# A score row copied later and value products in groups of four, in the stick-breaking attention of a streaming encoder step on one Trainium2 core

## What is computed

```python
def stick_breaking_block(q, k, v, q_pos, k_pos):
    z = jnp.einsum('bthd,bshd->bhts', q, k) * (SB_HEAD_DIM ** -0.5)
    mask = k_pos[None, :] < q_pos[:, None]
    log_fail = jnp.where(mask, jax.nn.log_sigmoid(-z), 0.0)
    after = lax.cumsum(log_fail, axis=3, reverse=True) - log_fail
    a = jnp.where(mask, jnp.exp(jax.nn.log_sigmoid(z) + after), 0.0)
    return jnp.einsum('bhts,bshd->bthd', a, v)
```

## Time and profile before

| | |
|---|---|
| median of 3 runs | 1090.89 us (1090.44 to 1092.22) |
| the profiled execution | 1091.26 us |
| its span, first to last instruction | 1089.4 us |
| mean granted TensorE clock | 0.995 |
| PE, DVE, ACT, POOL busy | 98%, 60%, 52%, 12% of the span |
| the stage of attention steps of the second pair | 241 to 325 us |

### The profile page before, as it was taken

How to read it: one execution, slowest core, us unless ns; L and a number is a source line. 1 busy time by engine, 2 the same in 40 slices (tenths; PEclk the granted TensorE clock), 3 DMA queues, 4 the chain that set the end, 5 groups by cost and what they waited for, 6 DMA issues and landing times.

```text
span 1089.4 us, 16617 instructions
## 1 busy us (share of the span) xinstructions
PE 1064.0 (98%) x6260; PEld 974.8 (89%) x6260; DVE 650.7 (60%) x1139; ACT 571.7 (52%) x1264; POOL 133.6 (12%) x145
## 2 busy tenths in 40 slices
PE   8999999999999999999999999999999999999995
PEld 5998779998779998779998779999999999999994
DVE  6677798387798377797387797335522231362117
ACT  4557884467883467883567884554022123252221
POOL 0001102011112011012011012001200110121220
PEclk9999999999999999999999999999999999999997
DMA  8041032132031132031142140153111111111144
GB/s 295 1 130 49 20 109 63 57 97 96 20 127 50 62 96 86 23 136 40 61 112 70 39 135 24 40 187 109 39 39 39 40 45 52 39 40 40 39 193 174
DMA packets 41487, 84.86 MB, mean 78 GB/s; under 512 B 2112, under 2 KB 22208, under 8 KB 41280
## 3 DMA queue, kind: packets, MB, share of 16 engines
q1 hardware_dynamic: 40832, 81.43, 22.9%
q10 hardware_dynamic: 576, 2.36, 0.6%
HBM read 67.27 MB, written 16.52 MB: 77 GB/s over the span
## 4 chain that ended last, share of the span: by engine, by line
PE 78%; ACT 9%; DVE 9%; issue 3%; DMA 1%; ACTq 0%; POOL 0%; DVEq 0%; SPq 0%; POOLq 0%
PE bank L671 50%; PE bank L1012 9%; DVE E L1676 3%; PE bank L808 3%; ACT E L1298 2%; ACT SPH L1310 2%; PE bank L838 2%; ACT E L1293 2%; DVE E L1680 1%; PE bank L794 1%; PE bank L681 1%; PE bank L708 1%; PE bank L912 1%; PE bank L954 1%; PE bank L976 1%
## 5 line engine op out<-in xcount | busy, mean ns | idle before, releaser
L671 PE MATMUL bank<-xh,wh 128*128 128x384 f32 x1296 | 438.8, 339 | 3.1 <-issue 2.8
L671 PE MATMUL bank<-xh,wl 128*128 128x384 f32 x1296 | 439.8, 339 | 0.0
L671 PE MATMUL bank<-xl,wh 128*128 128x384 f32 x1296 | 439.2, 339 | 0.0
L671 PEld LDWEIGHTS bank<-xh,wh 128*128 128x128 f32 x1296 | 243.6, 188 | 11.2 <-issue 9.3
L671 PEld LDWEIGHTS bank<-xh,wl 128*128 128x128 f32 x1296 | 243.6, 188 | 4.5 <-issue 2.0
L671 PEld LDWEIGHTS bank<-xl,wh 128*128 128x128 f32 x1296 | 243.5, 188 | 3.2 <-issue 0.2
L1183 ACT ACTIVATE slot<-bank,ngate 128x384 f32<-128x384 f32 x48 | 27.7, 576 | 177.9 <-PE bank L671 175.3
L1450 DVE CAST wh<-wr 128x1024 fp32r<-128x1024 f32 x64 | 43.7, 683 | 99.0 <-PE bank L671 98.1
L1455 DVE TENSOR_TENSOR wl<-wr,wh 128x1024 fp32r<-128x1024 f32 x64 | 90.8, 1419 | 1.9
L1676 DVE SCALAR_TENSOR_TENSOR E<-E,bank 128x512 f32<-128x512 f32 (+3 forms) x96 | 53.1, 553 | 47.7 <-ACT E L1298 47.6
L1858 DVE TENSOR_TENSOR slot<-bank,slot 128x384 f32<-128x384 f32 x24 | 13.4, 556 | 96.6 <-PE bank L1012 96.6
(11 more groups left out here) (226 smaller groups left out, 1687.0 us busy)
## 6 DMA issues: line engine op xcount, KB each, us to landing
wr<-wch SPq DMA_DIRECT2D x64, 512.0 KB, 3.6
KTc<-ckT SPq DMA_DIRECT2D x4, 2048.0 KB, 9.6
Vc<-cv SPq DMA_DIRECT2D x4, 2048.0 KB, 8.3
graw<-gated SPq DMA_DIRECT2D x8, 576.0 KB, 7.7
xres<-xT SPq DMA_DIRECT2D x1, 4608.0 KB, 15.7
yT<-yb SPq DMA_DIRECT2D x6, 576.0 KB, 3.0
xw<-xT SPq DMA_DIRECT2D x4, 768.0 KB, 11.6
okT<-kT ACTq DMA_DIRECT2D x4, 576.0 KB, 3.0
```

The lines of the kernel that those rows point to most:

```text
L671: i = nc.tensor.matmul(CH[n % 2][:, 0:WIN], weights[:, k, :], rows[:, k, w * WIN:(w + 1) * WIN], start=(m == 0), stop=(m == 23))
```

## The change

On ACT the copy of the score row leaves its place between exponential and logarithm. It now stands behind the high part of the softplus, waits for the softplus of its own step (`s_sp`, in steps without a high part too), and has a semaphore (`s_zr`), for which PE waits before it adds into the bank. The four row buffers `zr` become two tiles `zrows`, used at partitions 0 and 32 in turn; the high and low part of the carried row change places in `RT` in the same rhythm. In the space won, the weight tiles `Aw` go from three to five buffers; ACT waits for the value products of the step five before, and not three. PE makes the value products in groups of four, at steps 6, 10, 14, 18, 22 and 26, instead of groups of two at every even step from 4. The same instructions are issued, in other places; `s_hg` is waited for in five steps instead of two, at the same value.

```diff
--- before.py
+++ after.py
@@ -314,9 +314,9 @@
         SPH = [take(f"SPH{i}", [P, QW], F32R)[0] for i in range(2)]
         SPL = [take(f"SPL{i}", [P, QW], F32R)[0] for i in range(2)]
         RT = [take(f"RT{h}", [P, QW], F32R)[0] for h in range(2)]
-        zr = [take(f"zr{i}", [P, QW])[0] for i in range(4)]
-        aw_o = off[0] + 4 * QW
-        Aw = [take(f"Aw{i}", [P, QW])[0] for i in range(3)]
+        zrows = [take(f"zrows{i}", [P, QW])[0] for i in range(2)]
+        aw_o = off[0] + 3 * 4 * QW
+        Aw = [take(f"Aw{i}", [P, QW])[0] for i in range(5)]
 
         place = over(bt_o)
         Es = place("Es", [P, 2, SW])
@@ -426,6 +426,7 @@
         s_sp1 = sem("softplus_raw")
         s_sp = sem("softplus")
         s_S = sem("later_row")
+        s_zr = sem("first_key_row_copied")
         s_rz = sem("later_rows_zeroed")
         s_sph = sem("softplus_high")
         s_spl = sem("softplus_low")
@@ -514,6 +515,18 @@
         s_yo = sem("y_done")
         s_out = sem("y_stored")
 
+        def row_at(n):
+            return 32 * (n % 4 // 2)
+
+        def zr(n, cols):
+            return zrows[n % 2][row_at(n):row_at(n) + 1, cols]
+
+        def row_high(n, cols):
+            return RT[STEPS[n][2]][row_at(n):row_at(n) + 1, cols]
+
+        def row_low(n, cols):
+            return RT[STEPS[n][2]][32 - row_at(n):33 - row_at(n), cols]
+
         def need(eng, s, v):
 
             if v > 0:
@@ -811,9 +824,11 @@
                         if q == 0:
                             pe.wait_ge(s_cr, 3)
                             pe.wait_ge(s_sp, t + 1)
+                            pe.wait_ge(s_zr, SUMS * p + sums_until(m))
                             i = add(negtri, E[m % 2], c0)
                         else:
                             pe.wait_ge(s_sph, SPLITS * p + rows_until(m))
+                            pe.wait_ge(s_zr, SUMS * p + sums_until(m))
                             add(negtri_r[:, :], SPH[m % 2], c0)
                             pe.wait_ge(s_Sl, SUMS * p + sums_until(m - 2))
                             add(rows_r[:, :], RT[h], row_col(m - 2))
@@ -822,22 +837,21 @@
                         i.then_inc(s_cum, 1)
                     for x in B_PIECES[n][mid:]:
                         product(4 + 8 * p + x // 9, x // 3 % 3, x % 3)
-                    if n >= 4 and n % 2 == 0:
-                        wd, j, _ = STEPS[n - 4]
-                        c0 = first_col(n - 4)
-                        if n == 4:
+                    if n >= 6 and n % 4 == 2:
+
+                        if n == 6:
                             need(pe, s_oc, 3 * p)
                             pe.wait_ge(s_te, 6 * p + 3)
-                        if j == 4 * wd + 3:
-                            need(pe, s_gA, 2 * p + wd)
                         pe.wait_ge(s_a, NS * p + n - 2)
                         if diagonal(n - 3):
                             pe.wait_ge(s_am, DIAGS * p + diagonals_until(n - 3))
-                        for h in range(2):
-                            r = slice(DH * h, DH * h + DH)
-                            nc.tensor.matmul(OB[r, c0:QW], v_nat[:, j * P + DH * h:j * P + DH * h + DH],
-                                             Aw[(n - 4 + h) % 3][:, c0:QW], start=(j == 4 * wd + 3), stop=(j == 0),
-                                             skip_group_check=True).then_inc(s_av, 1)
+                        for m in range(n - 6, n - 2):
+                            wd, j, h = STEPS[m]
+                            c0, r = first_col(m), slice(DH * h, DH * h + DH)
+                            if j == 4 * wd + 3 and h == 0:
+                                need(pe, s_gA, 2 * p + wd)
+                            nc.tensor.matmul(OB[r, c0:QW], v_nat[:, j * P + DH * h:j * P + DH * h + DH], Aw[m % 5][:, c0:QW],
+                                             start=(j == 4 * wd + 3), stop=(j == 0), skip_group_check=True).then_inc(s_av, 1)
                     for w12 in ended(B_PIECES[n - 2]) if n >= 2 else ():
                         turn_recurrence(p, w12)
                 for w12 in ended(B_PIECES[-2]) + ended(B_PIECES[-1]):
@@ -1291,28 +1305,29 @@
                         elif n >= 2:
                             act.wait_ge(s_spl, SPLITS * p + rows_until(n - 2))
                         nc.scalar.activation(E[n % 2][:, c0:QW], ZB[n % 4][:, c0:QW], ACT.Exp).then_inc(s_E, 1)
-                        if STEPS[n][1] > 0:
-                            need(act, s_Sl, SUMS * p + (sums_until(n - 4) if n >= 4 else 0))
-                            nc.scalar.activation(zr[n % 4][0:1, row_col(n):QW], ZB[n % 4][0:1, row_col(n):QW], ACT.Copy)
                         act.wait_ge(s_E, t + 1)
                         nc.scalar.activation(E[n % 2][:, c0:QW], E[n % 2][:, c0:QW], ACT.Ln, bias=1.0).then_inc(s_L, 1)
                     if 2 <= n <= NS + 1:
                         m = n - 2
                         c0, t = first_col(m), NS * p + m
                         act.wait_ge(s_cum, t + 1)
-                        need(act, s_av, t - 2)
-                        if m < 2:
+                        need(act, s_av, t - 4)
+                        if m < 5:
                             need(act, s_hg, 3 * p)
-                        nc.scalar.activation(Aw[m % 3][:, c0:QW], ZB[m % 4][:, c0:QW], ACT.Exp).then_inc(s_a, 1)
+                        nc.scalar.activation(Aw[m % 5][:, c0:QW], ZB[m % 4][:, c0:QW], ACT.Exp).then_inc(s_a, 1)
                     if n < NS and tile_rank(n) > 0:
                         c0, t = first_col(n), NS * p + n
                         act.wait_ge(s_sp, t + 1)
                         nc.scalar.activation(SPH[n % 2][:, c0:QW], E[n % 2][:, c0:QW], ACT.Copy).then_inc(s_sph, 1)
+                    if n < NS and STEPS[n][1] > 0:
+                        act.wait_ge(s_sp, NS * p + n + 1)
+                        need(act, s_Sl, SUMS * p + (sums_until(n - 4) if n >= 4 else 0))
+                        nc.scalar.activation(zr(n, slice(row_col(n), QW)), ZB[n % 4][0:1, row_col(n):QW], ACT.Copy).then_inc(s_zr, 1)
                     if 2 <= n <= NS + 1 and STEPS[n - 2][1] > 0:
                         m, cols = n - 2, slice(row_col(n - 2), QW)
                         act.wait_ge(s_rz, 2 * (p + 1))
                         act.wait_ge(s_S, SUMS * p + sums_until(m))
-                        nc.scalar.activation(RT[STEPS[m][2]][0:1, cols], zr[m % 4][0:1, cols], ACT.Copy).then_inc(s_Sh, 1)
+                        nc.scalar.activation(row_high(m, cols), zr(m, cols), ACT.Copy).then_inc(s_Sh, 1)
                     recurrence_aside(p, n)
                     for w12 in ended(B_PIECES[n]):
                         window_recurrence(p, w12)
@@ -1512,16 +1527,15 @@
             def later_row(p, m):
 
                 cols = slice(row_col(m), QW)
-                row = zr[m % 4][0:1, cols]
+                row = zr(m, cols)
                 dve.wait_ge(s_a, NS * p + m + 1)
                 V.tensor_tensor(row, ZB[m % 4][0:1, cols], row, ALU.subtract).then_inc(s_S, 1)
 
             def later_row_low(p, m):
 
-                h, cols = STEPS[m][2], slice(row_col(m), QW)
+                cols = slice(row_col(m), QW)
                 dve.wait_ge(s_Sh, SUMS * p + sums_until(m))
-                V.tensor_tensor(RT[h][32:33, cols], zr[m % 4][0:1, cols], RT[h][0:1, cols].bitcast(F32),
-                                ALU.subtract).then_inc(s_Sl, 1)
+                V.tensor_tensor(row_low(m, cols), zr(m, cols), row_high(m, cols).bitcast(F32), ALU.subtract).then_inc(s_Sl, 1)
 
             def values_low(p):
 
@@ -1933,7 +1947,7 @@
                         m = n - 2
                         c0 = first_col(m)
                         pool.wait_ge(s_a, NS * p + m + 1)
-                        G.tensor_tensor(Aw[m % 3][:, c0:c0 + P], Aw[m % 3][:, c0:c0 + P], causal, ALU.mult).then_inc(s_am, 1)
+                        G.tensor_tensor(Aw[m % 5][:, c0:c0 + P], Aw[m % 5][:, c0:c0 + P], causal, ALU.mult).then_inc(s_am, 1)
                     for w12 in ended(B_PIECES[n]):
                         window_recurrence(p, w12)
```

## The result

The changed kernel takes **1117.1 us** (median of 4 runs, 1116.69 to 1117.58) against 1091.4 (1090.44 to 1092.22) for the kernel before on the same chip. The ratio is 1.0236, 95% interval 1.022 to 1.0251. The forecast was 1100.3, the range 1090.5 to 1105: the direction is right, the size is not. 25.7 us were lost where 9.4 were forecast.

What follows compares the result with a forecast made beforehand. ACT and DVE were taken to set the pace together from step 2 to 20, PE after. Per pair 0.68 + 0.67 + 0.40 + 0.29 + 0.3 = 2.34 us, 9.4 in four: 1090.89 + 9.4 = 1100.3 us, range 1090.5 to 1105.

Steps and rivals of the forecast that it cites:

- The sum of the late copy: Attention stage: copy +0.13 us net per step, plus waits; 2.04 us later per pair at step 20, 2.34 in all.
- The stall of steps 8 and 9: ACT: the late copy waits for the masked softplus; exponential 10 comes 1.35 us later, 0.67 of it new.
- the 0.6 for late low parts: Steps 21 and 25: PE arrives earlier and waits for the row's later low parts, 0 to 0.6 us, 0.6 taken.
- so I take the same price (bounds 0 and 0.1 us per row, off ACT's path): Rows at partition 32: same price as before, since the low part written there takes 0.68 against 0.67 us.
- each instruction overlaps the next by 0.10: ACT: the copy added behind the high part costs its duration minus 0.10 us, 0.47 at 512 columns.
- Behind step 20: PE -0.3: Value groups of steps 20 and 24 go, saving PE 0.3 us per pair that is sure to be time.
- The groups before step 20: Larger value groups there shorten PE where it waits for others; PE work falls 1.3 us per pair in the whole stage.
- a break costs: PE: a break between the two kinds of matmul costs 0.10 + 0.11 + 0.05 = 0.26 us.
- four records one behind the other at 0.23: PE: a group of two value products is four records, 0.92 us at the usual 0.23, of 1.01 measured.
- PE sets the pace: Rival: the saved breaks count whole, 5.4 us faster, 1085.5 us; chance 0.15.
- Worse than the sum: Rival: PE also waits for the copy before adds and for rows in steps 15 to 19; above 1104 us; chance 0.05.
- The signs I had named: Exponential to logarithm 0.60 us, copy waits 0.8 and 0.3, groups 1.97, PE waits +3.6 per pair, chunk 3's first window 2 later.

Runs made afterwards that it cites:

- P and C: Changed kernel (late copy, rows at partitions 0 and 32 in turn, five weight buffers) with value products in groups of two again: 1113.7 us.
- C alone: Kernel before with the row copied behind the high part; rows at partition 0, groups of two, three weight buffers: 1098.9 us, ratio 1.0072.
- the halves above: Late copy, groups of two, all rows at partition 32, with each ScalarE row instruction split into two halves of its columns: 1135.2 us, one run.
- P alone: Kernel before with rows at partitions 0 and 32 in turn, five weight buffers; copy in its old place, groups of two: 1105.9 us, ratio 1.0139.
- all rows at 32: Kernel before with rows at partition 32 in every step, copy in its old place, groups of two: 1121.8 us; with the late copy 1124.2.

## Why the prediction was wrong, point by point

- **The sum of the late copy was right up to step 20.** Alone it measured 7.6 us, 1.9 per pair; the sum had 2.04 up to step 20, and 0.6 behind it. Against the kernel before, from step 2's exponential, exponential 8 came 0.62 later (sum 0.68), exponential 10 1.36 later (1.35), the row's low part in step 18 1.95 later (2.04 in all), and chunk 3's first window 1.95 later. The stall of steps 8 and 9 measured 2.7 / 4 = 0.68 per pair (0.67). Behind step 20 nothing was added: the stage is 1.95 longer in all, and the 0.6 for late low parts was not there.
- **The step that failed: "so I take the same price (bounds 0 and 0.1 us per row, off ACT's path)"**, for rows at partition 32. It put at nothing what measured 14.6 us alone. I priced the duration of the instruction and named DVE alone. The duration is in fact nearly the same (0.57 to 0.59 us for the copy, 0.61 to 0.63 for the row's high part); the price is at the joints, and on ACT's own path: two lost overlaps of 0.12 to 0.14 us per step. P and C against C alone, the exponentials come 0.28 later with each step that has a copy and a high part: 1.1 us over steps 2 to 5 and 3.3 over steps 10 to 21. At the last exponential it is 4.5 us per pair; 0.7 of it disappears in PE's slack at the stage's end, and 14.8 / 4 = 3.7 are left. The sum used "each instruction overlaps the next by 0.10" as a constant, when the rows had shown it only for neighbours at the same partition.
- **It could be read before.** In the earlier trace rows the row's low part, written at partition 32, ends at 248.14, and the next instruction starts at 248.17; the clamp after that starts at 249.32, 0.08 before its predecessor's end at 249.40. The Trainium skill, VectorE: DVE Perf Modes, Two Vector instructions with no wait between them, says that a VectorE instruction is held until all earlier ones have finished when its input or output starts in another group of 32 partitions than the last one in the same memory. The trace agrees for VectorE, with the 0.03 after the end and the 0.08 before it just named, and the halves above show the same of ScalarE, for which the page does not say it.
- **"Behind step 20: PE -0.3" failed too.** The group at step 24 does go, but its products return behind the last wait, where nothing hides them: +0.86 per pair. I had taken PE to set the pace there; with 4.5 us of delay ahead of it ACT and DVE set it to the very end. The view to read was PE's order behind the last wait, not the work in total.
- **The groups before step 20** saved more PE work than I said, and it was no time, as I said. A group of four at 512 columns takes 1.87 us to the next product (334.55 to 336.42), where two groups of two take 2.02. So a break costs 0.10 + 0.11 + 0.15 = 0.36 us and not 0.26, and is worth nothing where PE waits. My reading of the earlier trace rows as four records one behind the other at 0.23 was wrong: they start two at a time, 0.48 apart (0.43 inside a group of four), with 0.52 from the last two to the next kind of product. The Trainium skill, TensorEngine Tiling (Array Packing), Key Properties, says that tiles can work in parallel; the trace agrees, with 1.01 us for two heads' products against 1.00 for one.
- **Rivals.** "PE sets the pace" (1085.5) fell. "Worse than the sum" gave the right side, but through "over 3.3 us per pair" from other causes; it had 0.05, too little for a case that holds every unpriced wait.
- **The signs I had named** came in part: 0.60 from exponential to logarithm, 0.72 and 0.19 idle before the copies of steps 8 and 9 (0.8 and 0.3). Groups of four take 1.87 and not 1.97. PE's idle time in the lines of the scores and sums grows by 6.1 us in the second pair (1.2 to 7.3), not 3.6; with C alone by 1.6. And chunk 3's first window, which should have come 2 us later, came 5.57 later: it starts at 312.46, 64.24 behind step 2's exponential (248.22), where the kernel before has 301.07 - 242.40 = 58.67. PE's view there, for the earlier trace rows:

```profile
310.84 0.40 PE L821 MATMUL bank<-SPL,negtri_r 128*128 128x512 f32 x1
312.46 0.41 PE L684 MATMUL bank<-xh,wh 128*128 128x384 f32 x1 [1.22 <-issue]
```

Open: in P alone and with all rows at 32 the share of ACT's starts was not taken apart from DVE's as it was for P and C, and why three lost overlaps cost 8.4 us each and the others 7.3 to 7.7. Not tried: the copy in ACT's idle time ahead of the high part.

## What to carry to other kernels

When a one-row tile moves to another partition, look at the starts of its neighbours, not at its duration: on a chain of short instructions the lost overlap, 0.12 us at each change, can be dearer than the copy that was moved. Where two engines pace each other, work pays to move only in the steps where the receiver idles, so ask for its idle time step by step. And before a group of instructions is made larger, find the last wait of the stage: what stands ahead of it is hidden as long as the engine has idle time there, what comes to stand behind it is time.

## What the runs showed of the hardware that I had not expected

- ScalarE overlaps an ACTIVATE with the one before it by 0.09 us only if source and destination begin in the same group of 32 partitions as before; else it starts 0.02 to 0.03 behind its end: from the start of a 1x512 row's copy to the next start it is 0.60 instead of 0.48 us. It is the change that costs: two instructions in a row that both read and both write where the one before did, at partition 32 too, overlap.
- VectorE shows the same: in full-width steps the subtraction of a row at partition 0 starts 0.60 to 0.61 us behind the clamp's start, that of a row at partition 32 0.71 to 0.72.
- The value products of two heads, 64 columns of the array each, run at the same time: a group of two takes 1.01 us, a group of one 1.00. Going over from products of 128 columns to such a group and back costs PE 0.36 us.
- TensorE's mean granted clock was 0.994 to 0.996 in the profiled executions of all these kernels, also with PE 5% idle, in pauses of up to 1.2 us in the stage.
